# Norm chains, forgetful attention's statistics and a memset put in another order in a two-block Trainium2 kernel

## The chip, the cores and the metric

The kernel runs on one core of one Trainium2 chip. The metric is the device time of one execution in microseconds (us), taken as the median of several runs. Everything is float32; the host does no arithmetic.

## What is computed

Two blocks of two layers each work on `x`, 256 tokens of width 1024. The first block's layer is

```
h     = rmsnorm(x, norm_g) * (1 + scale) + shift          # shift, scale, gate = silu(c) @ w_ada + b_ada
proj  = h @ w_in                                          # retention, SSD, attention parts and gates
ret   = rmsnorm_per_head(retention(rq, rk, rv)) * silu(rg)        # 4 heads of 128
ssd   = rmsnorm(ssd_scan(conv(xbc), dt) * silu(z), ssd_norm_g)    # 16 heads of 64
fox   = forgetting_attention(fq, fk, fv, log_f) * silu(fg)        # 8 heads of 64, causal softmax
x     = x + gate * (concat(ret, ssd, fox) @ w_out)
```

After it comes a final norm with gain `final_g`. The second block's layer also has 256 context tokens, which it updates in its first layer only:

```
mod   = silu(c) @ ada_w + ada_b                           # six vectors, for x and for the context
h     = rmsnorm(x, norm1_w) * (1 + sc1) + sh1
mix   = (sigmoid gates) * (conformer_conv(h), mLSTM(h), grouped_attention(h)) @ w_out
        # attention norms queries and keys per head of 64, then rotates them
x     = x + g1 * mix
x     = x + g2 * conv_ffn(rmsnorm(x, norm2_w) * (1 + sc2) + sh2)
```

## The kernel before

**Layout.** Tokens stand along the free axis, channels on the 128 partitions: `xT` is 8 tiles (`KT`) of 128x256, `xcT` 8 tiles of 128x512 with the context in its first 256 columns. A product keeps float32 precision by three matmuls over split numbers: high by high, low weight by high, high weight by low, each 8 matmuls for a tile of 128 output channels; these 24 are one strip (`split_strip`, whose instructions all carry line 741, the helper `mm`). A few projections, where precision comes from plain float32 matmuls, aren't split (`project_tok`).

**Weights.** SyncE's queue (SP) loads slots of 1 MB, one after another, into a ring of 5 places; a slot is loaded when the one that had its place before is used (`load_slot`). A slot has two halves. ScalarE (ACT) copies a half rounded to fp32r into one of three `w_high` buffers (`high_parts`, L1484), which waits until the strip three halves back is through, and VectorE (DVE) subtracts it from the raw half for the low part (L1983, `weights_low_out` L2207, `low_part` L2336); GpSimd (POOL) makes some (L1917).

**Conditioning.** The vectors `mod` come from pairs of slots ("ada" pairs, `ada`) that are spread over the layers: `conditioning_pairs` names for each pair a host slot, and PE does the pair in `take` of its host, in front of it. ScalarE and VectorE finish a batch of pairs (`ada_out`, `mod_out`, `ada_mod` L1959/L1963).

**Order.** Every engine has its own list of instructions, written out by hand. Engines meet only on semaphores: `step` counts an instruction's end, `wait_ge(when(name))` waits for it. So what stands behind a waiting instruction on its engine waits too. `unit` gives PE the next PSUM bank in rotation.

**A norm.** ScalarE squares the tiles (L1492 in the first block, L1658 to L1662 for the context, `x` and `x` times gain, L1683 in the second block); PE sums them over channels with `group_sum`, four column groups side by side, 64 columns each for 256 tokens; ScalarE takes the root (`rms_root`, L1437), for which it loads the table of Sqrt (ACT_TABLE_LOAD) as a rule; VectorE makes the reciprocal (L1968, L2280, L2298); PE spreads it to all partitions (`group_spread`, units `nb1` and `nb`); VectorE multiplies `x` by it (L1973, L2302, L2311 and L2313), and ScalarE applies gain and shift (L1504, L1691), upon which PE's projections start. `gain` is made from `mod` (L1976, L2287). In the first block the spread stands in `project_tok`, behind `take` of slot ("rv", l, 0), so behind its hosted pairs and its DMA. In the second block `high_parts` of the first halves stands between root and shift. The memset of `upad`, the feed-forward's padded tile (L2651, 128x4128), is VectorE's, between the residual and the reciprocal.

**Forgetful attention.** One iteration for each head h: PE turns the probabilities (`fox_turn`, L986 to L988), makes scores for head h+2, values for head h−1, and one strip of the output projection's first halves (`project_out`). VectorE makes logits (L2151, L2152) and probabilities (`fox_prob`, up to L2164), a low part of an output weight (L2207), and the tail work: `fox_out` (L2185), low tiles of the mixed input (`mixed_lows`, L2191) and the adds of a slot to `x` (`add_out`, L2222 to L2226). Behind head 0's strip, PE sums squares for the RMS of four retention heads and of SSD (`stats`): one-column matmuls with a column of ones, 10 results with tokens on partitions; VectorE takes the reciprocal `rstd_col` (128x10) at head 2, and PE spreads it in `spread`, at head 2 for SSD and at heads 5 and 6 for retention. After the loop come eight strips of the output projection's second halves.

**Block 2's first norm.** The context is loaded by SP in front of slot ("akv", 0, 0), when the last scores of layer 1's attention are made. Its squares, the squares of `x` and of `x` times gain are summed in this order; the root of the final norm (`rootg`) comes ahead of the context's (`rootc`).

**Query and key norm.** In the second block VectorE makes low parts 16 to 28 of the mixers' weights with depthwise conv taps between them (`early_taps`, L2365); behind part 26 it takes the reciprocal `qk_r` (L2430 to L2432), which PE spreads (`qk_spread`), and behind part 28 the five products of L2438, which PE's rotation waits for.

Of the kernel before, what the change touches and what calls it, by code (L numbers as in the profile page):

```python
# [29 lines left out]
P = 128  # L30
# [160 lines left out]
def conditioning_pairs():  # L191
# [25 lines left out]
    return order, hosted, gathered, settled  # L217

# [173 lines left out]
def program(nc, w, out, known):  # L392
# [4 lines left out]
    with ctx:  # L397
# [31 lines left out]
        smalls = sb("smalls", [P, N_SMALL])  # L429

# [90 lines left out]
        rstd_col = A(10)  # L521
# [145 lines left out]
        def _(sync):  # L667
# [48 lines left out]
        def _(tensor):  # L716
# [17 lines left out]
            def take(name):  # L734
                for n in ada_hosts.get(name, ()):
                    ada(n)
# [33 lines left out]
            def ada(n):  # L770

                batch, first = n // ADA_BATCH, n % ADA_BATCH * 2
                if first == 0:
# [3 lines left out]
                for m, slot in enumerate(pair_slots(ada_pairs[n]), first):  # L777
# [29 lines left out]
            def group_sum(u, x, n, t):  # L807

                w = n // 4
                for g in range(4):  # L810
                    i = mm(u[g * 32:(g + 1) * 32, 0:w], ones[:, 0:32], x[:, g * w:(g + 1) * w], t == 0, t == KT - 1)
# [9 lines left out]
            def first_layer(l):  # L821
                u = unit(("ssq1", l))
# [28 lines left out]
                def project_tok(part, n):  # L851
                    for s in range(n):
                        wt = take((part, l, s))
                        if (part, s) == ("rv", 0):
                            u = unit(("nb1", l))
                            pe.wait_ge(*when(("rms1", l)))
                            group_spread(u, rms1[:, 0:SEQ // 4], SEQ).then_inc(*pe.step(("full", ("nb1", l))))
# [141 lines left out]
                def stats():  # L999

                    u = unit(("stats", l), FOXO_BANKS)
                    for h in range(RET_HEADS):
                        pe.wait_ge(*when(("retsq", l, h // 2)))
                        for b in range(2):
                            mm(u[:, 2 * h + b:2 * h + b + 1], k1[:, h, b * P:(b + 1) * P], one_col)
                    for b in range(2):
                        for t in range(KT):
                            pe.wait_ge(*when(("usq", l, t)))
                            i = mm(u[:, 8 + b:9 + b], xconv[:, t, b * P:(b + 1) * P], one_col, t == 0, t == KT - 1)
                    i.then_inc(*pe.step(("full", ("stats", l))))  # L1010

                def spread(name, c0, n):
# [3 lines left out]
                    for c in range(n):  # L1016
                        i = mm(u[:, c * P:(c + 1) * P], rstd_col[:, c0 + c:c0 + c + 1].to_broadcast([P, P]), ident)
# [14 lines left out]
                for h in range(FOX_HEADS):  # L1032
# [8 lines left out]
                    if h == 2:  # L1041
                        spread(("ssdr", l), 8, 2)
                    if h in (5, 6):
                        spread(("retr", l, h - 5), 4 * (h - 5), 4)
# [12 lines left out]
            i.then_inc(*pe.step(("full", "ssqc")))  # L1057
            u, ug = unit("ssqf"), unit("ssqg")
# [5 lines left out]
            ig.then_inc(*pe.step(("full", "ssqf"), ("full", "ssqg")))  # L1064

            def second_layer(l):
# [4 lines left out]
                def norm(i2, lo):  # L1071
                    u = unit(("ssq2", l, i2))
# [3 lines left out]
                    i.then_inc(*pe.step(("full", ("ssq2", l, i2))))  # L1076

# [353 lines left out]
        def _(scalar):  # L1431
# [55 lines left out]

            def first_layer(l):
                g1 = f"p1_{l}"
                for t in range(KT):  # L1490
                    a.wait_ge(*when(("x1", l - 1, t) if l else "x_in"))
                    scalar.activation((xconv if l else h1)[:, t, :], xT[:, t, :], ACT.Square).then_inc(*a.step(("sq1", l, t)))  # L1492
                if l == 0:
                    a.wait_ge(*when("cst"))
# [122 lines left out]
                u_done(6)  # L1617
                u_done(7)
                mixing = ("wo1", l)
# [6 lines left out]

# [1146 lines left out]
```

## Time and profile before

| | us |
|---|---|
| median of 3 runs | 2445.13 (2444.18 to 2448.66) |
| the profiled execution | 2441.16 |
| its span, first to last instruction | 2439.3 |
| TensorE (PE) busy | 2332.0, 96% |
| VectorE (DVE) busy | 1408.3, 58% |
| ScalarE (ACT) busy | 970.9, 40% |
| GpSimd (POOL) busy | 117.7, 5% |
| mean granted TensorE clock | 0.97 of full speed |
| HBM read | 319.93 MB, 132 GB/s over the span |

Busy times are sums over the span. The chain of waits is followed back from the last instruction; its shares tell which engine the end waited for.

### The profile page before, as it was taken

What the parts mean: (1) busy time and instruction counts of PE and PEld (TensorE: products, weight loads), DVE (VectorE), ACT (ScalarE), POOL (GpSimd) and SP (SyncE); (2) the same over time, 40 slices, a digit from 0 to 9 for tenths busy, and PEclk for the clock granted to TensorE, in tenths of its full rate; (3) what the DMA queues carried; (4) which work ended last, traced back from release to release, by engine and by line L of the source; (5) the groups of instructions that cost most, each with busy time, mean ns of one, the idle gap of its engine ahead of it and who ended that gap; (6) DMA issues with size and microseconds to landing.
All of it is one profiled execution on the core that took longest, in us unless ns stands there. A gap on an engine that the chain in (4) does not pass through costs nothing.

```text
span 2439.3 us, 34769 instructions
## 1 busy us (share of the span) xinstructions
PE 2332.0 (96%) x14810; PEld 1937.9 (79%) x14810; DVE 1408.3 (58%) x2584; ACT 970.9 (40%) x1563; POOL 117.7 (5%) x95
## 2 busy tenths in 40 slices
PE   6999989999899999999999999999989899998999
PEld 3898778988767877776787677776877878898999
DVE  1467644665457767544344465655257656465995
ACT  2338533376433345352221333331244445543552
POOL 0000000000000022111000000000000132100000
PEclk8999899998899999999999999999989999999999
DMA  9784257962336111113332455322323221464553
GB/s 294 253 280 155 70 170 230 298 221 83 126 105 170 55 53 53 35 44 98 89 116 87 138 173 173 121 95 83 99 85 82 78 70 53 138 208 130 187 181 126
DMA packets 335531, 323.23 MB, mean 133 GB/s; under 512 B 28560, under 2 KB 334992, under 8 KB 335248
## 3 DMA queue, kind: packets, MB, share of 16 engines
q1 hardware_dynamic: 335376, 321.00, 41.6%
q8 instruction: 117, 1.92, 0.3%
q14 instruction: 38, 0.31, 0.1%
HBM read 319.93 MB, written 1.05 MB: 132 GB/s over the span
## 4 chain that ended last, share of the span: by engine, by line
PE 85%; DVE 7%; ACT 4%; DMA 3%; issue 1%; POOL 0%; SPq 0%; ACTq 0%
PE ps L741 84%; ACT w_high L1484 1%; DMA ring<-w_in 1%; DVE parts L1983 1%; DMA ring<-w_ada 1%; DVE arena L2365 1%; PE ps L1238 1%; POOL parts L1917 0%; DVE parts L2336 0%; ACT arena L1843 0%; DMA xcT<-ctx_t 0%; DVE arena L2126 0%; DVE arena L2120 0%; DVE parts L2330 0%; SPq L672 0%
## 5 line engine op out<-in xcount | busy, mean ns | idle before, releaser
L741 PE MATMUL ps<-parts,w_high 128*128 128x256 f32 (+1 forms) x6384 | 1141.8, 328 | 6.0 <-DVE parts L2330 2.2
L741 PEld LDWEIGHTS ps<-parts,w_high 128*128 128x128 f32 x6384 | 957.8, 191 | 135.6 <-issue 24.4
L741 PE MATMUL ps<-parts,parts 128*128 128x256 f32 (+1 forms) x3384 | 608.9, 322 | 13.9 <-DVE parts L2207 5.7
L1484 ACT ACTIVATE w_high<-ring 128x1024 fp32r<-128x1024 f32 (+2 forms) x426 | 433.3, 1027 | 440.2 <-PE ps L741 343.1
L741 PEld LDWEIGHTS ps<-parts,parts 128*128 128x128 f32 x3384 | 505.1, 191 | 67.5 <-DVE parts L2207 6.1
L2336 DVE TENSOR_TENSOR parts<-ring,w_high 128x1024 fp32r<-128x1024 f32 (+2 forms) x262 | 304.1, 1168 | 242.6 <-ACT w_high L1484 242.4
L1917 POOL TENSOR_TENSOR parts<-ring,w_high 128x512 fp32r<-128x512 f32 x88 | 116.9, 1354 | 1985.8 <-ACT w_high L1484 1985.7
L741 PE MATMUL ps<-arena 128*64 128x256 f32 (+7 forms) x928 | 183.0, 397 | 3.5 <-ACT arena L1813 3.5
L741 PEld LDWEIGHTS ps<-arena 128*128 128x128 f32 (+2 forms) x928 | 123.6, 171 | 51.9 <-issue 29.4
L2365 DVE SCALAR_TENSOR_TENSOR arena<-arena,cols 128x512 f32<-128x512 f32 (+1 forms) x240 | 159.7, 665 | 6.1
L1983 DVE TENSOR_TENSOR parts<-ring,w_high 128x1024 fp32r<-128x1024 f32 x88 | 104.9, 1221 | 95.4 <-ACT w_high L1484 95.4
L1895 ACT ACTIVATE arena<-ps 128x512 f32<-128x512 f32 (+1 forms) x88 | 43.2, 491 | 239.4 <-PE ps L741 239.4
L741 PE MATMUL ps<-arena,ring 128*128 128x512 f32 (+1 forms) x304 | 99.3, 486 | 0.0
L741 PE MATMUL ps<-ring,csel 128*32 128x256 f32 x1152 | 76.7, 410 | 20.9 <-DMA ring<-w_ada 20.1
L741 PEld LDWEIGHTS ps<-arena,ring 128*128 128x128 f32 x304 | 57.5, 190 | 38.5 <-issue 34.4
L741 PE MATMUL ps<-arena,cst 128*32 128x64 f32 (+7 forms) x428 | 66.2, 364 | 19.5 <-DVE arena L2298 7.0
L741 PE MATMUL ps<-ring,hT 128*128 128x256 f32 (+1 forms) x384 | 73.9, 355 | 7.5 <-ACT hT L1504 7.5
L1856 ACT ACTIVATE arena<-ps,cols 128x512 f32<-128x512 f32 (+1 forms) x48 | 27.8, 580 | 129.3 <-PE ps L741 128.1
L741 PEld LDWEIGHTS ps<-ring,csel 128*32 128x32 f32 x1152 | 35.5, 116 | 54.5 <-DMA ring<-w_ada 17.7
L741 PEld LDWEIGHTS ps<-ring,hT 128*128 128x128 f32 x384 | 65.1, 197 | 16.8 <-ACT hT L1504 7.8
L741 PE MATMUL ps<-w_high,parts 128*128 128x256 f32 x512 | 69.7, 288 | 1.1 <-ACT arena L1771 0.7
L741 PEld LDWEIGHTS ps<-w_high,parts 128*128 128x128 f32 x512 | 63.3, 190 | 8.1 <-issue 4.2
(266 smaller groups left out, 1833.9 us busy)
## 6 DMA issues: line engine op xcount, KB each, us to landing
ring<-w_in SPq DMA_DIRECT2D x118, 1024.0 KB, 5.3
ring<-ada_w SPq DMA_DIRECT2D x48, 1024.0 KB, 6.0
ring<-ffn_w_up SPq DMA_DIRECT2D x44, 1024.0 KB, 5.1
ring<-w_ada SPq DMA_DIRECT2D x24, 1024.0 KB, 7.3
ring<-w_out SPq DMA_DIRECT2D x16, 1024.0 KB, 5.2
ring<-ffn_w_down SPq DMA_DIRECT2D x16, 1024.0 KB, 5.1
ring<-w_out SPq DMA_DIRECT2D x16, 512.0 KB, 4.1
ring<-w_mlstm_out SPq DMA_DIRECT2D x8, 1024.0 KB, 5.1
```

The source lines that it names most:

```text
L741: return tensor.matmul(o, a, b, start=first, stop=last)
L1238: i = tensor.transpose(u[:, kb * P:(kb + 1) * P], att_p[:, n % 2, b, kb * P:(kb + 1) * P], ident)
L1484: scalar.activation(half_high(m), half_raw(m), ACT.Copy).then_inc(*a.step(("w_high", m)))
L1856: scalar.activation(sgt[:, n // 2 % 2, n % 2, lo:TT], bank(("bg", l, b, t))[:, lo:TT], ACT.Sigmoid, bias=col(g2, "branch_gate_b_2")[:, gat ...
L1895: scalar.activation(o, bank((name, l, t))[:, lo:TT].rearrange("p (a b) -> p a b", b=SEQ), ACT.Copy).then_inc(*a.step(("upad", l, s, part, ...
L1917: gpsimd.tensor_tensor(half_low(n)[:, part, :], half_raw(n)[:, part, :], half_high(n)[:, part, :].bitcast(F32), ALU.subtract).then_inc(*p. ...
L1983: vector.tensor_tensor(half_low(n), half_raw(n), half_high(n).bitcast(F32), ALU.subtract).then_inc(*v.step(("w_low", n)))
L2336: vector.tensor_tensor(half_low(n), half_raw(n), half_high(n).bitcast(F32), ALU.subtract).then_inc(*v.step(("w_low", n)))
L2365: vector.scalar_tensor_tensor(out=o, in0=x, scalar=wk, in1=o, op0=ALU.mult, op1=ALU.add).then_inc(*v.step(("dw", l, t, k), *((("cacc", l, ...
```

## The change

`load_root` is new on ScalarE: a Sqrt over one column, in front of a norm's squares. The spread `nb1` leaves `project_tok`: in layer 0 it stands between pairs 2 and 3, in layer 1 behind the sums. VectorE makes the gains of layer 1 ahead of its norm. At three slots (`AMID_NORMS`) the hosted pair is done in halves, one in front of the group sums and one behind them, and each of these slots' second pair gets another host. `stats` uses `group_sum` with 64 columns for each of the five statistics and `spread` uses `group_spread`; `rstd` is 128x320. VectorE's order in attention's head and tail, ScalarE's high parts there, the place of the context's load, the order of `rootc` and `rootg`, and the order of the query and key norm change. The memset of `upad` goes to GpSimd in two parts (2864 and 1264 columns).

```diff
@@ conditioning_pairs
-    hosts += [("rv", 1, 0), ("rv", 1, 0), ("rq", 1, 0), ("rk", 1, 0)]
+    hosts += [("rv", 1, 0), ("rv", 1, 1), ("rq", 1, 0), ("rk", 1, 0)]
-    hosts += [("akv", 0, 0), ("akv", 0, 0), ("mk", 0, 0), ("mk", 0, 1)]
-    hosts += [("upa", 0, 0), ("upa", 0, 0), ("upa", 0, 1), ("upa", 0, 2)]
+    hosts += [("akv", 0, 0), ("cug", 0, 0), ("mk", 0, 0), ("mk", 0, 1)]
+    hosts += [("upa", 0, 0), ("upg", 0, 0), ("upa", 0, 1), ("upa", 0, 2)]
+AMID_NORMS = (("rv", 1, 0), ("akv", 0, 0), ("upa", 0, 0))
@@ SyncE
-                if slots[n][0] == ("akv", 0, 0):
+                if slots[n][0] == ("wo", 1, DEPTH - 1, 3, 1):
                     sp.wait_ge(*when(("full", ("foxs", DEPTH - 1, FOX_HEADS - 1))))
                     load("ctx_in", xcT[:, :, 0:CTX], w["ctx_t"], "ctx_in")
@@ TensorE
+            def amid_norm(name, half):
+                for n in ada_hosts.get(name, ()):
+                    ada(n, (half,))
@@ first_layer
+                if l:
+                    amid_norm(("rv", l, 0), 0)
                 u = unit(("ssq1", l))
...
+                if l:
+                    amid_norm(("rv", l, 0), 1)
+                else:
+                    ada(2)
+                u = unit(("nb1", l))
+                pe.wait_ge(*when(("rms1", l)))
+                group_spread(u, rms1[:, 0:SEQ // 4], SEQ).then_inc(*pe.step(("full", ("nb1", l))))
                 if l == 0:
-                    ada(2)
                     ada(3)
                     ada_sum(0)
@@ stats
                     for h in range(RET_HEADS):
                         pe.wait_ge(*when(("retsq", l, h // 2)))
-                        for b in range(2):
-                            mm(u[:, 2 * h + b:2 * h + b + 1], k1[:, h, b * P:(b + 1) * P], one_col)
-                    for b in range(2):
-                        for t in range(KT):
-                            pe.wait_ge(*when(("usq", l, t)))
-                            i = mm(u[:, 8 + b:9 + b], xconv[:, t, b * P:(b + 1) * P], one_col, t == 0, t == KT - 1)
+                        group_sum(u[:, h * w:(h + 1) * w], k1[:, h, :], SEQ, 0, 1)
+                    for t in range(KT):
+                        pe.wait_ge(*when(("usq", l, t)))
+                        i = group_sum(u[:, RET_HEADS * w:(RET_HEADS + 1) * w], xconv[:, t, :], SEQ, t)
@@ spread
-                        i = mm(u[:, c * P:(c + 1) * P], rstd_col[:, c0 + c:c0 + c + 1].to_broadcast([P, P]), ident)
+                        i = group_spread(u[:, c * SEQ:(c + 1) * SEQ], rstd[:, c0 + c, :], SEQ)
@@ ScalarE
+            def load_root():
+                scalar.activation(spare[:, :], eps, ACT.Sqrt, scale=1.0, bias=eps).then_inc(*a.step())
@@ GpSimd
+            def pads(l):
+                part = MV_AT - FT * TT
+                p.wait_ge(*when(("madd", l, 3 * KT - 1)))
+                gpsimd.memset(upad_flat[:, part:], 0.0).then_inc(*p.step())
+                p.wait_ge(*when(full(("wo2", l, KT - 1))))
+                gpsimd.memset(upad_flat[:, 0:part], 0.0).then_inc(*p.step(("upads", l)))
@@ VectorE, attention's head and tail
-                fox_logits(1)
                 fox_prob(0)
+                ssd_low(5)
+                fox_logits(1)
...
-                fox_out(3)
-                mixed_lows(8, 9, 10, 11, 14, 15)
+                mixed_lows(8, 9, 10, 11, 14)
+                weights_low_out(9)
+                fox_out(3)
+                mixed_lows(15)
                 add_out(2, 0)
+                weights_low_out(10)
                 add_out(3, 0)
@@ VectorE, query and key norm
-                for n in range(16, 29):
+                for n in range(16, 27):
                     low_part(mix_half + n)
-                    early_taps(4)
-                    if n == 26:
+                    if n == 24:
                         v.wait_ge(*when(("qk_root", l)))
...
+                for n in range(27, 29):
+                    low_part(mix_half + n)
+                    early_taps(4)
@@ VectorE, norm of the feed-forward
-                v.wait_ge(*when(("merged", l, KT - 1)))
-                vector.memset(upad_flat, 0.0).then_inc(*v.step(("upads", l)))
                 norm(1, lo)
+                split_high("up", ("h2", l, 1), lo)
                 low_part(half_no[("upg", l, 0), 0])
```

## Rows read from the trace of the kernel before

**Rows 1.** The page: span, busy times of engines, shares of the chain.

```profile
span 2439.3 us, 34769 instructions
...
PE 2332.0 (96%) x14810; PEld 1937.9 (79%) x14810; DVE 1408.3 (58%) x2584; ACT 970.9 (40%) x1563; POOL 117.7 (5%) x95
...
PE 85%; DVE 7%; ACT 4%; DMA 3%; issue 1%; POOL 0%; SPq 0%; ACTq 0%
```

**Rows 2.** Windows: stretch, length, busy and instructions by engine, granted clock, DMA.

```profile
257.90:264.70 6.80, 6.80 (x28) 5.96 (x28) 5.30 (x14) 6.74 (x14) 0.00 (x0) 0.50 0.01 2
...
286.67:292.43 5.76, 5.76 (x40) 4.62 (x38) 3.52 (x10) 2.70 (x7) 0.00 (x0) 1.00 0.00 1
...
1909.90:1913.30 3.40, 3.40 (x38) 3.40 (x35) 2.45 (x5) 0.00 (x0) 0.00 (x0) 0.50 0.02 5
```

**Rows 3.** PE timeline, attention's head, layer 0: start, duration, form, wait before.

```profile
256.82 0.33 PE L986 MATMUL ps<-cst,arena 128*128 128x128 f32 x1 [1.34 <-DVE arena L2164]
...
264.76 7.18 PE L741 MATMUL ps<-cst,arena 128*128 128x1 f32 x48
...
280.46 0.27 PE L986 MATMUL ps<-cst,arena 128*128 128x128 f32 x1
...
292.43 0.27 PE L986 MATMUL ps<-cst,arena 128*128 128x128 f32 x1
```

**Rows 4.** PE timeline: group sums of a norm; a spread of rstd.

```profile
342.92 0.88 PE L741 MATMUL ps<-arena,cst 128*32 128x64 f32 x48
...
622.61 1.05 PE L741 MATMUL ps<-cst,arena 128*128 128x128 f32 x8
```

**Rows 5.** PE timeline, attention's tail, layer 0.

```profile
322.05 1.55 PE L741 MATMUL ps<-parts,parts 128*128 128x256 f32 x8 [2.86 <-DVE parts L2207]
323.40 3.28 PE L741 MATMUL ps<-parts,w_high 128*128 128x256 f32 x16
```

**Rows 6.** PE timeline, first norm of layer 0.

```profile
37.53 1.97 PE L741 MATMUL ps<-arena,cst 128*128 128x64 f32 x8
...
43.25 1.22 PE L741 MATMUL ps<-ring,hT 128*128 128x256 f32 x2 [3.75 <-ACT hT L1504]
```

**Rows 7.** PE timeline, first norm of layer 1.

```profile
344.55 3.63 PE L741 MATMUL ps<-ring,csel 128*32 128x256 f32 x64
348.83 1.10 PE L741 MATMUL ps<-arena,cst 128*128 128x64 f32 x8 [0.65 <-DMA ring<-w_in]
353.69 0.80 PE L741 MATMUL ps<-ring,hT 128*128 128x256 f32 x1 [3.76 <-ACT hT L1504]
```

**Rows 8.** ACT timeline, the same norm.

```profile
344.38 1.28 ACT L1437 ACT_TABLE_LOAD   x1
```

**Rows 9.** SP and PE timelines, block 2's first norm.

```profile
651.30 0.59 SPq L672 DMA_DIRECT2D xcT<-ctx_t  x1
...
660.96 8.23 PE L741 MATMUL ps<-arena,cst 128*32 128x64 f32 x192 [4.34 <-ACT arena L1658]
...
673.47 2.89 PE L741 MATMUL ps<-arena,cst 128*128 128x64 f32 x24
679.23 9.75 PE L741 MATMUL ps<-hT,ring 128*128 128x512 f32 x16 [2.87 <-ACT hT L1691]
```

**Rows 10.** PE timeline, query and key norm, both layers of block 2.

```profile
869.68 0.67 PE L741 MATMUL ps<-arena,cst 128*128 128x256 f32 x2 [2.27 <-DVE arena L2438]
...
1909.49 4.51 PE L741 MATMUL ps<-cst,arena 128*64 128x128 f32 x48 [2.16 <-DVE arena L2432]
...
1923.48 4.09 PE L741 MATMUL ps<-arena,cst 128*128 128x256 f32 x6 [3.55 <-DVE arena L2438]
```

**Rows 11.** DVE and PE timelines, the feed-forward's norm, layer 0.

```profile
1368.55 3.50 DVE L2651 MEMSET arena<- 128x4128 f32 x1 [0.81 <-issue]
...
1379.38 5.25 PE L741 MATMUL ps<-hT,ring 128*128 128x512 f32 x6 [5.25 <-ACT hT L1691]
```

**Rows 12.** POOL timeline, the kernel's start.

```profile
0.73 0.45 POOL L1908 MEMSET csel<- 128x424 f32 x1 [0.29 <-POOLq L2767]
```

More of the change, by code:

```diff
@@ L520, in program @@
         A.at = RETP_AT + 4 * SEQ
-        rstd_col = A(10)
+        rstd = A(5, SEQ // 4)
         X = Carve(xpad_at)
@@ L734, in take @@
             def take(name):
-                for n in ada_hosts.get(name, ()):
+                for n in () if name in AMID_NORMS else ada_hosts.get(name, ()):
                     ada(n)
@@ L768, in split_strip, with ada @@
                 return i
-            def ada(n):
+            def ada(n, halves=(0, 1)):
                 batch, first = n // ADA_BATCH, n % ADA_BATCH * 2
-                if first == 0:
+                if first + halves[0] == 0:
                     unit(("ada_y", batch), ADA_BANK)
@@ L776, in ada @@
                 last = 2 * ADA_BATCH - 1
-                for m, slot in enumerate(pair_slots(ada_pairs[n]), first):
+                for m, slot in [(first + half, pair_slots(ada_pairs[n])[half]) for half in halves]:
                     pe.wait_ge(*when(("slot", slot)))
@@ L853, in project_tok @@
                         wt = take((part, l, s))
[L854 to L857, printed above, removed]
                         u = unit((part, l, s))
@@ L1041, in first_layer @@
                     if h == 2:
-                        spread(("ssdr", l), 8, 2)
+                        spread(("ssdr", l), RET_HEADS, 1)
                     if h in (5, 6):
-                        spread(("retr", l, h - 5), 4 * (h - 5), 4)
+                        spread(("retr", l, h - 5), 2 * (h - 5), 2)
                 fox_values(FOX_HEADS - 1)
@@ L1642, in first_layer @@
                         u = bank(("stats", l))
-                        scalar.activation(rstd_col[:, 0:8], u[:, 0:8], ACT.Sqrt, scale=1.0 / RET_DH, bias=eps).then_inc(*a.step())
-                        scalar.activation(rstd_col[:, 8:10], u[:, 8:10], ACT.Sqrt, scale=1.0 / D, bias=eps).then_inc(*a.step(("rstd_root", l), read(("stats", l))))
+                        ret, ssd = rstd[:, 0:RET_HEADS, :].rearrange("p a b -> p (a b)"), rstd[:, RET_HEADS, :]
+                        scalar.activation(ret, u[:, 0:SEQ], ACT.Sqrt, scale=1.0 / RET_DH, bias=eps).then_inc(*a.step())
+                        scalar.activation(ssd, u[:, SEQ:SEQ + SEQ // 4], ACT.Sqrt, scale=1.0 / D, bias=eps).then_inc(*a.step(("rstd_root", l), read(("stats", l))))
                     if h == 4:
@@ L1685, in norm @@
                         rms_root(("ssq2", l, i2), rr[:, 0, 0:(TT - lo) // 4], D, ("root2", l, i2), 0, (TT - lo) // 4)
-                    high_parts(*((("mix", l), half_no[("cug", l, 0), 1]) if i2 == 0 else (("up", l), half_no[("upg", l, 0), 1])))
                     a.wait_ge(*when(("gain2", l, i2)))
@@ L1691, in norm @@
                             scalar.activation(hT[:, t, c0:c0 + 256], hT[:, t, c0:c0 + 256], ACT.Identity, scale=gain2[:, l, i2, t, st:st + 1], bias=mod2[:, l, i2 * 24 + t, st:st + 1]).then_inc(*a.step(("h2", l, i2, t)))
+                    high_parts(*((("mix", l), half_no[("cug", l, 0), 1]) if i2 == 0 else (("up", l), half_no[("upg", l, 0), 1])))
                 norm(0, 0, [(CTX, 0), (0, 1)])
@@ L1921, in back_lows @@
                         gpsimd.memset(mv[:, :, :, M_DH:M_DH + 1], 1.0).then_inc(*p.step(("mv_ones", l)))
+            def pads(l):
[4 more added lines that the diff above has]
+                gpsimd.memset(upad_flat[:, 0:part], 0.0).then_inc(*p.step(("upads", l)))
             for l in range(DEPTH):
                 back_lows(l)
+                pads(l)
         @block.vector
@@ L1966, in first_layer, with gains @@
                 g1 = f"p1_{l}"
+                def gains():
+                    ada_mod(1, l, 0, 24 if l else 16)
+                    v.wait_ge(*when(("mod", 1, l, 24 if l else 16)))
+                    vector.scalar_tensor_tensor(out=gain1[:, l, :], in0=mod1[:, l, 8:16], scalar=1.0, in1=col(g1, "norm_g"), op0=ALU.add,
+                                                op1=ALU.mult).then_inc(*v.step(("gain1", l)))
+                if l:
+                    gains()
                 v.wait_ge(*when(("root1", l)))
@@ L2178, in first_layer @@
                         ssd_low(t - 3)
+                fox_prob(0)
+                ssd_low(5)
                 fox_logits(1)
-                fox_prob(0)
                 def fox_out(t):
@@ L2228, in first_layer @@
                 ssd_out(7)
-                ssd_low(5)
+                ssd_low(6)
                 weights_low_out(0)
-                ssd_low(6)
                 ssd_low(7)
@@ L2242, in first_layer @@
                         v.wait_ge(*when(("rstd_root", l)))
-                        vector.reciprocal(rstd_col, rstd_col).then_inc(*v.step(("rstd_col", l)))
+                        vector.reciprocal(rstd, rstd).then_inc(*v.step(("rstd_col", l)))
                     if h in (3, 5, 7):
@@ L2260, in first_layer @@
                 for s in range(4):
-                    for n in range(9 + 2 * s, min(11 + 2 * s, 16)):
+                    for n in range(max(11, 10 + 2 * s), min(12 + 2 * s, 16)):
                         weights_low_out(n)
```

39 lines of the change are left out of this document (26 added, 13 removed).

## The prediction

> **What bounds the kernel now.** I read the page first: TensorE (PE) is busy for 2332.0 of the span's 2439.3 us and has 85% of the chain of waits [rows 1]. So time can go in three ways only: PE's waits (about 100 us, the gaps in PE's timeline summed), PE's own instructions, and PE's clock. The granted clock by windows shows the last one: in forgetful attention's head PE is busy without a pause and runs at 0.50, that is at 1.2 GHz, while the same loop two heads later runs at 1.00, 2.4 GHz [rows 2]. Such stretches follow a wait of PE nearly everywhere; there are 23 of them, 3.4 to 20 us long. I then read PE's timeline around each place that the diff touches, and the other engines' there to see what ends the wait. The sum is made against the profiled execution (2441.2 us, span 2439.3), which stands 4.0 below the median of the runs, 2445.13.
>
> **The change part by part.**
>
> Forgetful attention's head, both layers. Now PE waits 1.34 for VectorE's probabilities of head 0, then head 0 and 1 take 280.46 − 256.82 = 23.64 [rows 3], nearly all at half clock; 7.18 of it are the statistics, 48 one-column instructions of 150 ns. The change puts `fox_prob(0)` ahead of `fox_logits(1)` (and one `ssd_low` between): PE starts 1.34 earlier. The statistics become 96 instructions of 64 columns in four column groups. 48 of this kind took 0.88 at full clock [rows 4], so 96 take 1.8. A head with values takes 5.76 at full clock [rows 2]; head 0, with no values and with the statistics, 7.05. Sum: 23.64 − 7.05 − 5.76 = 10.8, and 1.34: 12.2; the same rows in layer 1 (570.16 to 594.11) give 12.5. I take −24.7 for both. This assumes full clock, since neither the wait nor the one-column instructions are left; the other end is −11.5 (rival A), and the best −27. VectorE's probabilities of head 1 are now due at 262.3, PE asks for them at 262.5: tight, worth 0.5 if late. Its reciprocal grows from 128x10 to 128x320, about 2.4 by the 128x128 one's 0.95; VectorE idles 4.1 in that iteration.
>
> Spreads. The rstd of heads and SSD is spread in pieces of 64 columns, 8, 16 and 16 instructions where there were 4, 8 and 8. Eight of the old took 1.05 [rows 4], eight of 64 columns 1.10 [rows 7]: a narrower one is not cheaper, so instructions count. Starts lie 0.12 apart: 20 more, +2.35 per layer, +4.7 (between +2, if pitch falls with the columns, and +6).
>
> Attention's tail, both layers. PE waits 2.86 (2.85 in layer 1) for low part 9, which VectorE makes behind the last values, six low tiles and the adds of two slots, and runs the next strips at half clock: 16 in 3.28 [rows 5], which at full clock are 1.64. The change makes low part 9 ahead of them, and low 10 between the adds. 2.85 + 1.65 = −4.5, twice: −9.0. At least the wait, −5.7, if the clock still falls; −9.5 at best.
>
> Start. PE issues the spread of rms1 at 37.53, after the last conditioning slot, and the first projection at 43.25, after 3.75 of wait [rows 6]: VectorE multiplies eight tiles in 2.74, then shift and gain. Now the spread is issued between slots at 31, where PE only waits for DMA, and those 2.74 lie there too. What stays is the sum (36.51 to 37.6), ScalarE's 0.18 and VectorE's two 0.17 (to 38.2 with the handovers) and 0.67 of ScalarE: PE starts at 38.9, −4.3. Its slots had landed by then. The other end is 0: the ring is the limit in layer 0 (rival B).
>
> First norm of layer 1. After PE's sum ScalarE loads its table, 1.28 [rows 8]; PE does four conditioning slots in 3.63, waits for DMA, spreads at 348.83, and starts at 353.69 after 3.76 [rows 7]. With the load in front of the squares, gains made before the chain and spread ahead of the slot's wait, it starts at 348.4 with both pairs, 1.8 of which now move to the next slot, where PE does them all the same: −5.3 + 1.8 = −3.5 (−0.5 to −4).
>
> Block 2's first norm. The context is issued at 651.30 and lands 9.2 later; PE waits 4.34 for its squares, sums in 8.23 paced by ScalarE's 24 squares, does four slots in 4.58, spreads at 673.47, waits 2.87, and starts at 679.23 [rows 9]. Issued before output slot (1,1,3,1) it lands near 625, inside attention's loop. SP's wait for the last scores stands ahead of that output slot now, and that slot's place is free at about the same time, so what it queues behind costs little. Then ScalarE has its context squares done before x1; 16 are left: 656.6 + 0.9 + 5.6 for the last, less what overlaps, sums end at 661; the table is loaded; two root and reciprocal steps to 662.5, spreads, 2.7 for tiles, the high parts no longer ahead: first matmul at 667. That is −12.2. The pair moved in front of "cug" (1.8) falls into a stall of PE on h's low parts. I take −11 (−6, if nb stays at half clock and SP is late, to −13).
>
> Query and key norm. Layer 0: PE waits 2.27, 0.65 and 0.22 for products that VectorE makes behind low parts 27 and 28, and 0.81 before the spread: −4.0. Layer 1: waits 2.16 and 3.55, and 48 instructions in 4.51 and six in 4.09 at half clock [rows 2, 10], where full gives 2.75 and 2.15: 2.16 + 1.76 + 3.55 + 1.94 = −9.3, less 0.1. VectorE idles enough there for the reciprocal to come two low parts sooner. Ends −8 and −14 for both.
>
> Norms of block 2 with the feed-forward. The memset of 3.50 stands between ScalarE's root and the reciprocal (1.3 to 1.9 late), the table load adds 1.28, the high parts 2.0: PE's wait of 5.25 [rows 11]. On GpSimd the memset is two pieces, by 128x424 in 0.45 [rows 12] 3.0 and 1.3, before the pads are read at 1383. PE starts near 1374.2: −5.2, with the pair now at "upg" +1.8: −3.4. Layer 1: −3.9; its first norm, load only: −0.75. Together −8.05 (−4 to −9).
>
> The sum is −24.7 + 4.7 − 9.0 − 4.3 − 3.5 − 11 − 13.3 − 8.05 = −69.2. Against it I set +5: waits of 2 to 4 us stay at five norms, and half-clock stretches of 3.4 us, each worth 1.7 to 3, may begin elsewhere. So −64: own time 2377, and 4 above it for the median, 2381. The likeliest case's own range is 2370 to 2389.
>
> **The rivals.**
>
> A. The clock stays at half in the head: PE needed no pause to be at 0.50 there [rows 2], so more than the wait may hold it down. For: the narrow score matmuls stay. Against: the same mix at 1.00 at 286.67. Price +6.6 per layer (head 0 and 1, 12.8 at full): 2394.
>
> B. Gains come back because slots arrive no sooner. For: the DMA digits are 9, 7 and 8 in the first slices; one slot was issued at 129.46 and landed 10.8 later. Against: PE's waits on w_in sum to only 0.6. Start, layer 1's norm and part of the tail are lost, +10: 2391.
>
> C. The memset on GpSimd stops VectorE. It is released by the last branch product, 1320.25, where VectorE's cast of 0.43 is next and PE already waits. If the two can't run beside each other, the cast is late by up to 3.0, in each layer: +6, 2387. No row of before has both at once. The Trainium skill ("SBUF — State Buffer", Who interferes with whom) says that VectorE's copies and casts may take a port pair that GpSimd shares, and that the first blocks the other; by it C would happen where the memset issues first.
>
> D. Slower than before: the clock stays at 1.2 GHz from attention's head through the output projection. Head 0 and 1 without the statistics take 8.2 each now, with values about 9, where full clock takes 5.76, and eight matmuls of a strip 2.0 for 1.04 (the output projection has 24 such): 8 × 3.3 and 24 × 1.0 per layer, +100 in all, 2481. It decides from +64 on, two thirds of it. For: 96 small instructions enter at the head. Against: 48 of them ran at full clock at 342.92 [rows 4].
>
> That the change doesn't do what it says, with gaps merely moved along (each queue serves what it served), would leave about −25: 2420.
>
> **How the numbers follow.** Forecast 0.58, A 0.15, B 0.11, C 0.08, gaps moved along 0.05, D 0.03. The range reaches from 2367, the better ends of head, tail and block 2, to 2405, two of A to C together with the worse ends of the norms. A measurement of this kernel can tell 0.2%, 5 us, from none. Faster: all but D and the worst of the fifth case, 0.96; same 0.01; slower 0.03.
>
> **What would show it.** In the changed trace: no wait before L986's successor, near 251 (everything being 4.3 earlier); statistics in 96 instructions of 1.8, at clock 1.00; no gap before low part 9's strip, and the clock at 1.00 behind it; the context landing before 630; PE's first projection at 38.9; memsets on GpSimd with VectorE's cast unmoved; block 2's projection some 12 us sooner after the last output strip; 0.3 at most before query and key products. The forecast is wrong if the clock row of the head says 0.50 (A), if waits on the ring appear in layer 0 (B), or if the total of PE's waits falls by less than 35.

## The result and the profile after

The changed kernel takes 2401.47 us (median of 4 runs, 2396.76 to 2405.11), against 2446.55 for the kernel before (4 runs, 2444.18 to 2448.66): a ratio of 0.9818, 95% interval 0.9802 to 0.9835, or 45 us less. Forecast were 2381 and 64 less; the range, 2367 to 2405, holds the time. Timed once more (x12 below) it gave 2400.26 and 0.9817 (0.980 to 0.9835). The profiled execution took 2404.85, which is 3 over its kernel's median; that of the kernel before, 2441.16, is 5 under its own.

The page of the changed kernel (span, busy times, chain), to be read beside [rows 1]:

```profile
span 2403.1 us, 35052 instructions
...
PE 2326.2 (97%) x14946; PEld 1926.4 (80%) x14946; DVE 1417.3 (59%) x2582; ACT 972.2 (40%) x1569; POOL 126.9 (5%) x99
...
PE 87%; DVE 6%; ACT 4%; DMA 2%; issue 1%; POOL 0%; SPq 0%; ACTq 0%; DVEq 0%
```

PE's waits fell from 100.8 to 71.2 us (its gaps over 0.3 us, summed), its busy time only by 6. The 6896 matmuls that read `w_high` come in the same order in both kernels, so the two traces can be laid side by side at each; the difference of their starts, read where it jumps, is the ledger of this case (profiled executions, 2441.2 and 2404.9; a place is read to some tenths of a us).

| place | forecast | measured |
|---|---|---|
| start | −4.3 | −3.0 |
| attention's head, 2 layers | −24.7 | −12.5, −12.4 |
| spreads, 2 layers | +4.7 | +2.15, +1.8 |
| attention's tail, 2 layers | −9.0 | −4.6, −4.3 |
| first norm of layer 1 | −3.5 | −3.4 |
| block 2's first norm | −11 | −12.9 |
| query and key norm | −13.3 | −3.6, −9.3 |
| other norms of block 2 | −8.05 | −3.1, −1.3, −3.8 |
| sum of the places | −69.2 | −70.3 |
| given back elsewhere | +5 | +34 |

So every place gave what was forecast within 2 us, and the miss is the last line. Its 34 hold for this pair of executions, which lie 36 apart; by the medians, 45 apart, 25 were given back, and x12's profiled execution, 40 apart, gives 30. Here is PE's timeline of the changed kernel at attention's head, at its tail, and at the norms, in the form of [rows 3] and of [rows 5 to 7] and [rows 9 to 11]:

```profile
30.11 1.97 PE L745 MATMUL ps<-arena,cst 128*128 128x64 f32 x8
...
39.16 6.03 PE L745 MATMUL ps<-ring,hT 128*128 128x256 f32 x15 [1.41 <-ACT hT L1528]
...
252.32 0.33 PE L999 MATMUL ps<-cst,arena 128*128 128x128 f32 x1
...
257.53 1.55 PE L745 MATMUL ps<-arena,cst 128*32 128x64 f32 x96
259.02 0.33 PE L999 MATMUL ps<-cst,arena 128*128 128x128 f32 x1
...
264.85 0.27 PE L999 MATMUL ps<-cst,arena 128*128 128x128 f32 x1
...
288.83 1.89 PE L745 MATMUL ps<-arena,cst 128*128 128x64 f32 x16
...
303.73 2.06 PE L745 MATMUL ps<-parts,w_high 128*128 128x256 f32 x16
...
327.78 1.10 PE L745 MATMUL ps<-arena,cst 128*128 128x64 f32 x8 [0.16 <-DVE arena L2016]
330.18 4.25 PE L745 MATMUL ps<-ring,hT 128*128 128x256 f32 x11 [1.30 <-ACT hT L1528]
...
631.83 8.61 PE L745 MATMUL ps<-hT,ring 128*128 128x512 f32 x16 [0.38 <-ACT hT L1719]
...
1335.67 6.60 PE L745 MATMUL ps<-hT,ring 128*128 128x512 f32 x13 [1.91 <-ACT hT L1719]
...
1866.33 2.84 PE L745 MATMUL ps<-cst,arena 128*64 128x128 f32 x48
...
1874.88 2.31 PE L745 MATMUL ps<-arena,cst 128*128 128x256 f32 x6
```

There is no wait ahead of the first turn any more, the statistics take 1.55, heads 0 and 1 end 12.53 after the first turn where they took 23.64 [rows 3], the 16 strip matmuls at the tail take 2.06 and wait for nothing, and the waits of 3.75, 3.76, 2.87 and 5.25 have become 1.41, 1.30, 0.38 and 1.91. The windows show the clock (busy times by engine, granted clock, DMA share): full in the head, half where new waits came.

```profile
252.00:257.50 5.50, 5.49 (x39) 4.32 (x35) 5.43 (x12) 5.47 (x12) 0.00 (x0) 1.00 0.45 158
...
1280.00:1286.80 6.80, 5.20 (x11) 3.79 (x12) 4.57 (x5) 0.00 (x0) 0.19 (x1) 0.50 0.09 31
2174.20:2181.10 6.90, 5.71 (x27) 5.50 (x26) 4.69 (x6) 1.06 (x1) 0.00 (x0) 0.51 0.09 28
```

In the profiled execution, what was given back is of three kinds, told apart in the ledger by whether a wait, the clock, or neither changed between two matched matmuls: 8 and 3 us for the two collisions (half clock behind them included), 10 for the clock elsewhere, 11 for the rate; 32 of the 34.

First, VectorE beside GpSimd. The cast of 0.43 that rounds the last tile of the merged branches and the new memset start together. DVE's, POOL's and PE's timelines of the changed kernel:

```profile
1277.68 2.79 DVE L2687 CAST parts<-arena 128x512 fp32r<-128x512 f32 x1
...
1277.71 2.48 POOL L1956 MEMSET arena<- 128x2864 f32 x1 [206.36 <-DVE arena L2683]
...
1280.53 0.79 PE L745 MATMUL ps<-parts,w_high 128*128 128x512 f32 x1 [2.71 <-DVE parts L2687]
```

The cast takes 0.3 more than the whole memset; PE waits 2.71 (2.84 in layer 1) where it waited 0.37 (0.47), here by PE's timeline of the kernel before:

```profile
1320.78 0.51 PE L741 MATMUL ps<-parts,w_high 128*128 128x512 f32 x1 [0.37 <-DVE parts L2634]
```

The same happens, not foreseen, in layer 1's attention: since the query and key norm ends sooner, VectorE's rotary steps (the rotation of queries and keys) and its two copies of the mLSTM's gate rows fall beside GpSimd's low parts. DVE's timeline, then POOL's and PE's, of the changed kernel:

```profile
1884.80 1.65 DVE L2510 TENSOR_TENSOR arena<-arena 128x512 f32<-128x512 f32 x1
1886.37 2.94 DVE L2447 COPY arena<-arena 4x512 f32<-4x512 f32 x2
...
1882.50 3.40 POOL L1946 TENSOR_TENSOR parts<-ring,w_high 128x512 fp32r<-128x512 f32 x2 [2.08 <-ACT w_high L1502]
...
1885.90 3.12 POOL L1946 TENSOR_TENSOR parts<-ring,w_high 128x512 fp32r<-128x512 f32 x2
...
1894.76 3.50 PE L745 MATMUL ps<-w_high,parts 128*128 128x256 f32 x16 [2.79 <-ACT arena L1800]
```

The four scores' maxima that VectorE takes behind the copies come late, ScalarE waits for the first of them, and PE for ScalarE. DVE's timeline of the kernel before at the same two copies:

```profile
1930.40 0.74 DVE L2397 COPY arena<-arena 4x512 f32<-4x512 f32 x2
```

Second, the clock. Half-clock stretches sum to 149.2 us before and 111.4 after (2 us of each lie behind the last instruction). The places of the table lost some 70 of them, so some 30 began elsewhere, 10 behind the new waits just shown and some 20 in places that are the same in both kernels, most of them at waits that were there before. PE's wait of 2.77 for ScalarE in layer 1's attention is one: it stands in both traces, here PE's timelines of the changed kernel and of the kernel before:

```profile
1963.44 3.68 PE L745 MATMUL ps<-arena 128*64 128x256 f32 x16 [2.77 <-ACT arena L1842]
```

```profile
2010.28 1.95 PE L741 MATMUL ps<-arena 128*64 128x256 f32 x16 [2.77 <-ACT arena L1813]
```

Only in the changed one do 10.2 us at half clock (1962.6 to 1972.9) come with it. But this is no property of the kernel alone: at the same wait of 2.77 the traces of x6 and x9 have 10.2, x12, the changed kernel once more, 6.8, x5 3.4, and x7 and x8 none. Twenty us at half clock are about 10 us of time.

Third, the rate at which full-clock matmuls follow one another, about 11 us; the two experiments below on addresses show it.

### The profile page after: what moved, and what is told of

Same layout as the page of the kernel before. It is cut to its first block, busy times and chain, and to the rows that moved or that the text cites. A ratio compares the mean times of both kernels' runs of the same rounds, so it can differ in the third digit from the quotient of the medians.

```text
span 2403.1 us, 35052 instructions
## 1 busy us (share of the span) xinstructions
PE 2326.2 (97%) x14946; PEld 1926.4 (80%) x14946; DVE 1417.3 (59%) x2582; ACT 972.2 (40%) x1569; POOL 126.9 (5%) x99
## 4 chain that ended last, share of the span: by engine, by line
PE 87%; DVE 6%; ACT 4%; DMA 2%; issue 1%; POOL 0%; SPq 0%; ACTq 0%; DVEq 0%
PE ps L745 86%; DVE parts L2030 1%; ACT w_high L1502 1%; DMA ring<-w_ada 1%; DMA ring<-w_in 1%; PE ps L1256 1%; POOL parts L1946 0%; ACT arena L1872 0%; DVE arena L2415 0%; DVE arena L2173 0%; DVE arena L2167 0%; DVE parts L2380 0%; DVE parts L2687 0%; ACT arena L1612 0%; SPq L676 0%
## 5 line engine op out<-in xcount | busy, mean ns | idle before, releaser
L745 PE MATMUL ps<-parts,parts 128*128 128x256 f32 (+1 forms) x3384 | 615.2, 323 | 7.7 <-POOL parts L1946 3.4
L745 PE MATMUL ps<-arena,cst 128*32 128x64 f32 (+7 forms) x700 | 74.8, 291 | 5.8 <-DVE arena L2348 3.4
L745 PEld LDWEIGHTS ps<-w_high,parts 128*128 128x128 f32 x512 | 64.6, 194 | 10.2 <-issue 4.2
```

Source lines behind the costliest of these rows:

```text
L745: return tensor.matmul(o, a, b, start=first, stop=last)
```

## The experiments

Each was timed against the kernel before in the same rounds. "Base" is the changed kernel at 0.9817 (x12). A difference of 0.0015 in the ratio, 3.7 us, is about the half width of one interval. Between two such ratios it is some 0.0023, 5 to 6 us: x1, x4, x8 and x9 are clear of the base, x3 just, x7 and x10 are not quite, x5 and x6 are not.

**x1: `spare` behind the arena.** The change allocates a one-column tile ahead of the arena.

```diff
-        spare = sb("spare", [P, 1])
         ...
         arena = sb("arena", [P, N_ARENA])
+        spare = sb("spare", [P, 1])
```

> The changed kernel, with the one-column tile `spare` allocated behind the arena instead of ahead of it, so that the arena (which holds most moving operands) starts at byte 120256 as before, and not at 120288. Address theory: matmuls in dense stretches start 1 to 3 per cent closer (FFN of layer 1: 116.9 ns from start to start as before, not 118.7; the 512-column ones in the first strips of block 2 227 ns, not 232), about 10 us less in all: near 2391 where the changed kernel has 2401. Rival (the slow drift is the chip's or the profile's, not the address's): same pitch, 118.7 and 232, and 2397 to 2405.

2387.03, ratio 0.9763 (0.9742 to 0.9785): 13 us less than the base, by moving one tile. Windows of dense full-clock strips in layer 1's feed-forward show the matmuls (first count) done in 150 us, in the kernel before, the changed one, and x1:

```profile
2282.00:2432.00 150.00, 150.00 (x1214) 147.45 (x1213) 118.88 (x218) 66.57 (x101) 0.00 (x0) 1.00 0.51 166
```

```profile
2242.00:2392.00 150.00, 150.00 (x1188) 147.47 (x1187) 118.14 (x216) 65.99 (x100) 0.00 (x0) 1.00 0.51 165
```

```profile
2228.00:2378.00 150.00, 150.00 (x1213) 147.44 (x1212) 118.55 (x218) 66.16 (x100) 0.00 (x0) 1.00 0.51 166
```

PE is busy for all of it in each, at clock 1.00, and does 26 matmuls fewer in the changed kernel alone. From start to start of neighbours that read `w_high` that is 117, 119 and 117 ns on average.

**x2: the kernel before with that tile, unused.**

```diff
         smalls = sb("smalls", [P, N_SMALL])
+        spare = sb("spare", [P, 1])
```

> The kernel before with nothing but an unused one-column tile ahead of the arena, which moves it by 32 bytes. Address theory: about 10 us slower than before, 2455 to 2458, with the changed kernel's pitches (118.7 ns in the FFN of layer 1) and the same waits as before. Rival: no difference, 2445 to 2448.

2455.66, ratio 1.0045 (1.0032 to 1.0059): 11 to 12 us slower, with nothing else changed. The same window does 1188 matmuls:

```profile
2297.00:2447.00 150.00, 150.00 (x1188) 147.47 (x1187) 117.04 (x214) 65.22 (x99) 0.00 (x0) 1.00 0.51 165
```

**x11: the same tile 16 columns wide, 64 bytes instead of 32.**

```diff
+        spare = sb("spare", [P, 16])
```

> The kernel before with an unused tile of 16 columns ahead of the arena, which moves it by 64 bytes instead of 32. Alignment theory (what costs is a start that is no multiple of 64 bytes): same as before, 2442 to 2447, pitch 116.9 ns in the FFN of layer 1. Rival (any shift against the tiles ahead of the arena, the ring and w_high, costs, or each address has its own pitch): 2450 to 2456.

2450.43 (12 runs, 2444.23 to 2461.47), ratio 1.0029 (1.0015 to 1.0043): my alignment theory falls. By stage the 64-byte shift goes both ways. Layer 1's feed-forward has a start each 120 ns (117 before, 119 with 32 bytes), block 2's first strips, of 512 columns, 231 (227, 232), while layer 0's feed-forward is faster than in the other four traces compared, 227 (231 to 232). Windows of layer 0's and layer 1's feed-forward in x11, then of layer 0's in the kernel before:

```profile
1446.00:1526.00 80.00, 80.00 (x425) 63.70 (x424) 46.99 (x62) 24.94 (x35) 0.00 (x0) 1.00 0.54 175
...
2287.00:2437.00 150.00, 150.00 (x1182) 147.47 (x1182) 117.41 (x215) 65.44 (x99) 0.00 (x0) 1.00 0.51 165
```

```profile
1440.00:1520.00 80.00, 80.00 (x418) 62.38 (x417) 45.57 (x61) 24.36 (x34) 0.00 (x0) 1.00 0.52 168
```

So where the arena starts changes the rate of a stage by up to 3% (117 to 120); which address suits which stage, and why, stays open.

**x3: GpSimd's first memset after the last cast.**

```diff
-                p.wait_ge(*when(("madd", l, 3 * KT - 1)))
+                p.wait_ge(*when(("h_high", "wo2", l, KT - 1)))
```

> The changed kernel, with GpSimd's first memset of the pad tile held until VectorE's last cast of the merged branches is done (it still wrote 2864 columns beside VectorE's tensor_tensor instructions). Port theory (cast and memset exclude each other): the cast is back at 0.43 and 0.29 us where it took 2.79 and 2.65, PE's wait before that strip falls from 2.71 and 2.84 to 0.4 and 0.5, and the time by 4.5 to 8 us (2.4 each and some half clock): near 2395. Rival (the cast was late for another reason, or the memset then delays the tensor_tensors that follow as much): within 1 us of the changed kernel.

2394.41, ratio 0.9792 (0.9777 to 0.9807): 6 us less. DVE's, POOL's and PE's timelines of x3:

```profile
1275.18 0.43 DVE L2687 CAST parts<-arena 128x512 fp32r<-128x512 f32 x1
...
1276.25 3.49 DVE L2386 TENSOR_TENSOR parts<-ring,w_high 128x1024 fp32r<-128x1024 f32 x3
...
1275.67 2.49 POOL L1956 MEMSET arena<- 128x2864 f32 x1 [208.40 <-DVE parts L2687]
...
1275.66 0.50 PE L745 MATMUL ps<-parts,w_high 128*128 128x512 f32 x1 [0.35 <-DVE parts L2687]
```

The cast is back at 0.43 and PE's wait at 0.35, and the three tensor_tensors beside the memset take 1.16 each as elsewhere. Rival C of the prediction is shown, with its price. The Trainium skill ("SBUF — State Buffer", Who interferes with whom) says that a cast or copy of VectorE can block on the port pair that GpSimd has, and that a VectorE instruction with two inputs in SBUF collides with a GpSimd instruction that reads but not with one that only writes. The traces agree on both: cast and memset exclude each other, tensor_tensor and memset don't (1.16), tensor_tensor and GpSimd's low parts do (1.65 for 0.69). Which of cast and memset issues first they don't settle: the cast's record starts 0.03 before the memset's in both layers, and it is the cast that is late.

**x4: statistics and spreads as before.** `stats`, `spread`, the two roots and the reciprocal are those of the kernel before.

```diff
-                        group_sum(u[:, h * w:(h + 1) * w], k1[:, h, :], SEQ, 0, 1)
+                        for b in range(2):
+                            mm(u[:, 2 * h + b:2 * h + b + 1], k1[:, h, b * P:(b + 1) * P], one_col)
...
```

> The changed kernel with the statistics and spreads of the kernel before (48 one-column instructions, spreads of 4, 8 and 8), all else as changed. Theory: the one-column instructions, which hardly use the array, make the clock fall to half in the head although PE no longer waits there: statistics 3.6 to 7 us instead of 1.6, the heads behind them at half clock, 9 to 16 us more over both layers, less 4 for the spreads: 2406 to 2413. Rival (the wait of 1.34 alone had made the clock fall): statistics 3.6 us at full clock, 2 more per layer, minus 2 for the spreads: no change in the sum, near 2401.

2412.25, ratio 0.9869 (0.985 to 0.9889): 12.7 us more. PE's timeline of x4:

```profile
257.31 5.42 PE L745 MATMUL ps<-cst,arena 128*128 128x1 f32 x48
...
267.58 2.08 PE L745 MATMUL ps<-parts,w_high 128*128 128x256 f32 x8
```

PE comes to the statistics at full clock, without a wait, and they take 5.42; half clock follows (262.7 to 269.5 in layer 0, 559.7 to 569.9 in layer 1), in which a strip's eight matmuls take 2.08 for 1.04. So the clock falls in the one-column instructions with no wait ahead of them.

**x5: VectorE's order in the head as before.**

```diff
+                fox_logits(1)
                 fox_prob(0)
-                ssd_low(5)
-                fox_logits(1)
...
```

> The changed kernel with VectorE's order in attention's head as before (logits of head 1 ahead of the probabilities of head 0), statistics and all else as changed. Theory (the one-column statistics set the clock, the wait does not): PE waits 1.3 us before the first turn again and the head stays at 2.4 GHz, statistics 1.6 us: 1.3 to 1.8 us more per layer, 2401 to 2405. Rival (the wait sets the clock as much): half clock over head 0, another 3 to 6 us per layer: 2408 to 2416.

2404.19, ratio 0.9830 (0.9815 to 0.9845), 3 us more, less than the times can tell; the trace has to. PE's timeline of x5:

```profile
253.41 0.33 PE L999 MATMUL ps<-cst,arena 128*128 128x128 f32 x1 [1.34 <-DVE arena L2211]
...
255.69 1.91 PE L745 MATMUL ps<-parts,w_high 128*128 128x256 f32 x8
```

In the trace it costs 2.8 at each head: 1.34 of wait and 3.4 us at half clock behind it (255.0 to 258.4, and 552.0 to 555.4 in layer 1). So the clock falls behind the wait too, for a shorter time; both theories were right in part. Of the head's 12.5 per layer the order gave about 2.8, the statistics by x4's time 6.3 and the 2.0 that their wider spreads cost, 11.1 together; x4's own trace has 6.4 and 8.4 at the two heads. What is left, 1 to 3 us, neither gave alone.

**x6 and x9: the context's load.** In x6 the load alone is put back in front of slot ("akv", 0, 0), in x9 the second pair's host too.

```diff
-                if slots[n][0] == ("wo", 1, DEPTH - 1, 3, 1):
+                if slots[n][0] == ("akv", 0, 0):
```

```diff
-    hosts += [("akv", 0, 0), ("cug", 0, 0), ("mk", 0, 0), ("mk", 0, 1)]
+    hosts += [("akv", 0, 0), ("akv", 0, 0), ("mk", 0, 0), ("mk", 0, 1)]
```

> The changed kernel with the context loaded where it was, in front of slot (akv, 0, 0). Theory of the prediction: of the 12.9 us that block 2's first norm gave, most is the context's landing: PE waits for context squares 3 to 4 us again, sums are paced by all 24 squares, ScalarE's root waits: 7 to 11 us more, near 2409. Rival (the table load, the order of the roots and the high parts gave most of it): 2 to 4 us more, near 2402 to 2404.

> The changed kernel with the context's load in front of slot (akv, 0, 0) and with both conditioning pairs hosted there again, as before (each still done in halves around the sums). With the load alone put back, the trace showed it issued at 604.0, since the slot itself now comes two places sooner; with both put back it should be issued near 615 and land near 624 or later. Theory (slot order and the load's place are two ways to one end): PE waits for context squares again, 6 to 9 us more at this place than in the changed kernel, 2406 to 2410. Rival (the context's landing was never worth much; table, roots and high parts were): 1 to 4 us more, 2400 to 2404.

x6: 2404.43, ratio 0.9831 (0.9816 to 0.9846); x9: 2410.34, ratio 0.9855 (0.9835 to 0.9875), 9 us over the base. SP's timeline shows why x6 did nothing at the place: the context is issued at 604.03, and ScalarE, which starts its squares at 614.8, doesn't wait for it. The changed kernel issues it at 580.81, earlier than anybody needs it.

```profile
604.03 0.59 SPq L676 DMA_DIRECT2D xcT<-ctx_t  x1
```

In x9 it is issued at 615.95, ScalarE starts its squares at 624.1, when it has landed, and PE waits for them, by PE's timeline:

```profile
624.58 2.59 PE L745 MATMUL ps<-arena,cst 128*32 128x64 f32 x64 [3.36 <-ACT arena L1685]
```

The strips behind are 4.4 to 7.3 late. So the prediction was right that the landing matters and wrong about which edit moves it: taking the second pair away from the slot moves slot and load two places forward in SP's queue, and the edit of the load on top of it adds nothing that can be told. Whether the load's edit would have been enough with both pairs in place wasn't tried, nor what gives the rest of the 12.9 at this place (the order of the roots, the table load, the high parts).

**x7: query and key norm as before.**

```diff
-                for n in range(16, 27):
+                for n in range(16, 29):
                     low_part(mix_half + n)
-                    if n == 24:
+                    if n == 26:
...
```

> The changed kernel with the query and key norm in its old order, in both layers. By the ledger of the two traces the new order gave 4.0 and 9.3 us at its place; against it, in layer 1, VectorE's rotary steps and the two copies of gate rows now run beside GpSimd's low parts (copies 1.50 us each instead of 0.41) and PE waits 2.79 instead of 0.69 at the first value strip, with 3.4 us of half clock behind it. Net theory: +13.3 less 2.1 + 1.7: 8 to 11 us more, 2408 to 2412. Rival (the gain comes back in full behind the place): within 3 us of 2400.

2406.16, ratio 0.9837 (0.9822 to 0.9852): 5 us more, under the range of 8 to 11 that I gave. In the trace the places lose 5.5 and 7.4, about the 13 of the forecast. Behind them 3.1 come back, as the wait of 2.79 on ScalarE is gone, and 5.1 more, as the 10.2 us of half clock at 1962.6 don't occur. The first is the port conflict's price; the second can't be put down to the order, since the length of this stretch changes between traces of kernels that have the same order.

**x10: no early table load, at any of its three calls.**

```diff
-                load_root()
...
```

> The changed kernel without the early Sqrt on ScalarE (the tile for it stays, so that the arena lies as in the changed kernel). Theory of the prediction: the table load of 1.28 us comes back between PE's sum and the root at five of the six norms (not at the start, where PE waits for slots): 1.0 to 1.3 us each and a little half clock, 5 to 8 us more, 2406 to 2409. Rival (PE has conditioning slots to do behind the sums, which hide the load): 1 to 3 us more.

2405.21, ratio 0.9837 (0.982 to 0.9855): 5 us more, at the edge of what the intervals can tell and at the low end of what was expected. The trace has less. PE's waits grow by 0.7 at layer 1's first norm, by 0.8 at block 2's first, and by 0.8 and 0.9 at the two norms of block 2's second layer, 3.2 in sum; at the norm ahead of the first feed-forward the load of 1.28 falls into time in which ScalarE is idle anyway, and costs nothing. At block 2's first norm the half clock is 3.4 us shorter than in the changed kernel's trace, so the strips behind are no later. Nothing of the 3.2 is left at the end: this profiled execution took 2404.85, as the changed kernel's did. So the trace stands nearer to the rival, and the 5 of the medians aren't settled.

**x12: the changed kernel again.** 

> The changed kernel itself once more, as the base that the single undone parts are read against: 2396 to 2405, 0.980 to 0.9835 of before.

2400.26 (4 runs, 2399.43 to 2401.14), ratio 0.9817 (0.980 to 0.9835). Its profile has 96.8 us of half clock, against 111.4 in the profile above, with the same waits (71.8 and 71.2).

**x8: three repairs together.** x1 and x3, and the two copies of gate rows put ahead of low part 27, where GpSimd is idle.

```diff
                 early_taps(DW_T * DW_K)
-                gate_rows()
...
+                gate_rows()
                 for n in range(27, 29):
                     low_part(mix_half + n)
```

> The changed kernel with three repairs together: `spare` behind the arena, GpSimd's first memset behind the last cast of merged branches, and the two copies of gate rows ahead of low part 27, where GpSimd is idle. If the three add up: 13 (address) + 6.5 (memset) + 2 to 4 (gate rows, with the half clock behind the wait): 2377 to 2381. If the gate rows' copies only move the conflict (the rotary steps still run beside GpSimd's reads): 2380 to 2384.

2373.93 (2372.86 to 2376.26), ratio 0.9709 (0.9694 to 0.9724): 26 us under the changed kernel and 3 below the low end that I gave, 2377. In the same rounds the kernel before took 2443.40, so this version gains 69.5. PE's waits are 65.3, half clock 79.4. The wait of 2.79 in layer 1's attention is back at 0.69 as in the kernel before, with no half clock, although the rotary steps still take 1.64 beside GpSimd; PE's timeline of x8:

```profile
1876.58 2.17 PE L745 MATMUL ps<-w_high,parts 128*128 128x256 f32 x16 [0.69 <-ACT arena L1800]
```

This is the fastest of the versions.

## Why the prediction came out as it did

**What bounds the kernel, and the terms.** Right: the sum of the places, −69.2, was measured as −70.3, and each term is within 2 us. The tail, the start and the norms of block 2 behind its first rest on the ledger; no run undid them by themselves. The half clock in the head went with the statistics (x4) and to a lesser part with the wait (x5), as assumed; rival A did not occur, and neither did D: the clock is at 1.00 in the head and behind it. The narrower spread was not cheaper, as read from [rows 7]. At the start PE began at 39.16 (forecast 38.9), but then ran at half clock for 5.2 us instead of 3.0, hence −3.0.

**The allowance.** This is the step that failed: "+5" for all that may come back, against +34 in the profiled executions and +25 by the medians. Its parts, by the ledger and the runs:

- Addresses, about 11 in the ledger, 13 by x1 and 12 by x2. The prediction dealt with the table load that writes `spare` and not with the 32 bytes by which its place moves the arena. It had no row for that, and no bound.
- Rival C, priced 6 with a chance of 0.08 and left out of the sum: 6 by x3, 8 in the ledger. It was the best bounded of the rivals: in the trace of before the cast starts 0.04 behind the product that was to release the memset.
- The same collision in layer 1's attention, about 3 by the ledger, with a wait 2.1 longer and half clock behind it. The prediction had looked for who is late when an engine is moved later, and not what an engine moved earlier meets.
- Half clock elsewhere, some 10 in the profiled execution, less in others (x12 has 15 us less of it, which is 7 of time). This alone, and the waits left at norms, the allowance was meant for.

The first three are 22 of the 25 that the medians give back, and with them repaired x8 gains 69.5, close to the sum of the places. One of the prediction's own signs was met and shows the same: it calls itself wrong if PE's waits fall by less than 35, and they fell by 29.6. The three waits that the collisions made longer hold 6.8 of that; without them the fall is 36.4. And "VectorE's cast unmoved", which it expected to see, failed (2.79 for 0.43). That 2401 lies in the range is partly luck: the range was to be filled by two of A to C with the worse ends of the norms, but the norms came at their good ends, only C occurred, and the largest part is the address, which isn't in it.

**The context.** Right in size, wrong in which edit does it (x6, x9). It also lands at 586.4, much before the 625 of the forecast, which nobody needs.

**Rival B and the fifth case.** Rival B did not occur: no wait on the ring came up in layer 0. A part of the gains did come back, but through clock, port and address, and not because queues served what they had served.

## What to carry to other kernels

When work is moved to another engine, look at what it will run beside, step by step: a memset that nothing waits for at that point stopped a cast of 0.43 us that the whole chain waited for. A new tile, however small, that moves large ones is a change of its own, to be timed by itself; put behind them, as in x1, it leaves their addresses alone. And a gain summed from waits and half clock can be given back in part: half clock came up in places where nothing had been changed, and by different amounts from one trace to the next.

## What the runs showed of the hardware

- An unused 4-byte-wide tile ahead of the arena, which moves it by 32 bytes, costs 0.45% (0.32 to 0.59, x2): matmuls start each 119 instead of 117 ns, and the 512-column ones each 232 instead of 227 in block 2's first strips, at a busy PE and full clock. 64 bytes (x11) are slower in three stages and faster in one (227 for 231 to 232).
- VectorE's cast and GpSimd's memset don't run beside each other: 2.79 for 0.43, with a memset of 2.48. GpSimd's tensor_tensor stretches VectorE's copy from 0.41 to 1.50 and a tensor_tensor from 0.69 to 1.65. Its memset leaves VectorE's tensor_tensor at 1.16 (x3).
- 48 one-column matmuls begun at full clock take 5.42, and 7 to 10 us at 1.2 GHz follow (x4); 96 matmuls of 64 columns in four column groups take 1.55, and the clock stays at 2.4 GHz.
- The same wait of 2.77 goes with 0 to 10.2 us of half clock in eight traces, and with 10.2 and 6.8 in two of the same kernel.
- A memset of 2864 columns takes GpSimd 2.48, where the row of 424 in 0.45 [rows 12] had suggested 3.0.
